# Down products of an FFN's last two tiles by blocks of tokens, and three RMS/layer norms worked block by block

## What is computed

```python
def swiglu(x, w_gu, w_down):
    gate, up = jnp.split(x @ w_gu, 2, axis=-1)
    return (jax.nn.silu(gate) * up) @ w_down
...
    h = h + 0.5 * swiglu(rms_norm(h, ffn1_norm[l]), ffn1_w_gu[l], ffn1_w_down[l])
    ...
    h = h + 0.5 * swiglu(rms_norm(h, ffn2_norm[l]), ffn2_w_gu[l], ffn2_w_down[l])
return rms_norm(h, final_norm)
...
x = post_norm(x, 0.5 * swiglu_2(x, ffn1_w_in[i], ffn1_w_out[i]), ln_g[i, 0], ln_b[i, 0])
```

## Time and profile before

| | |
|---|---|
| median of 3 runs | 1808.95 us (1808.13 to 1809.66) |
| the profiled execution | 1820.9 us, of which its span 1819.6 us |
| mean granted TensorE clock | 0.97 of full speed |
| PE busy | 1721.6 us, 95% of the span |
| DVE busy | 1193.8 us, 66% |
| ACT busy | 878.9 us, 48% |
| POOL busy | 92.3 us, 5% |
| DMA | 301.59 MB, mean 166 GB/s |

### The profile page before, as it was taken

One profiled execution on the slowest core, in us unless ns is written; L12 is line 12 of the kernel. 1 busy time (PEld: TensorE's weight loads), 2 busy tenths in 40 slices (PEclk: granted clock), 3 DMA queues, 4 the chain that ended last, 5 costly groups with the idle time before them and its releaser, 6 DMA issues.

```text
span 1819.6 us, 24706 instructions
## 1 busy us (share of the span) xinstructions
PE 1721.6 (95%) x9936; PEld 1489.1 (82%) x9936; DVE 1193.8 (66%) x1949; ACT 878.9 (48%) x1507; POOL 92.3 (5%) x123
## 2 busy tenths in 40 slices
PE   7999998989999999989999999799998998999995
PEld 6888897878888888888778888688888887888884
DVE  5766658837666666655757666666666674576665
ACT  5444546545444544455545454454443564454453
POOL 0000002210000000002210000100000000100000
PEclk9999998999999999999989999899998998999997
DMA  8545362025545454444425545355544232464531
GB/s 340 203 178 199 116 237 112 36 93 197 202 180 198 172 199 183 161 156 150 157 102 219 203 179 185 127 186 191 185 173 150 106 115 99 155 229 184 193 131 46
DMA packets 31970, 301.59 MB, mean 166 GB/s; under 512 B 3808, under 2 KB 4336, under 8 KB 5872
## 3 DMA queue, kind: packets, MB, share of 16 engines
q1 hardware_dynamic: 31856, 300.01, 44.8%
HBM read 298.93 MB, written 1.06 MB: 165 GB/s over the span
## 4 chain that ended last, share of the span: by engine, by line
PE 82%; DVE 10%; ACT 5%; issue 1%; POOL 1%; DMA 0%; SPq 0%; DVEq 0%; ACTq 0%
PE bank L402 28%; PE bank L392 25%; PE bank L391 11%; PE bank L381 7%; DVE w_lo L354 3%; PE bank L394 2%; ACT w_hi L347 1%; DVE x L663 1%; POOL rstd L771 1%; DVE x L687 1%; PE bank L434 1%; PE bank L448 1%; PE bank L449 1%; PE bank L964 1%; PE bank L1392 1%
## 5 line engine op out<-in xcount | busy, mean ns | idle before, releaser
L354 DVE TENSOR_TENSOR w_lo<-w_raw,w_hi 128x1024 fp32r<-128x1024 f32 (+5 forms) x545 | 607.1, 1165 | 265.3 <-ACT w_hi L347 265.1
L392 PE MATMUL bank<-xT,w_hi 128*128 128x512 f32 x1920 | 674.1, 396 | 1.0 <-DVE w_lo L354 0.9
L347 ACT ACTIVATE w_hi<-w_raw 128x1024 fp32r<-128x1024 f32 (+5 forms) x561 | 523.8, 995 | 150.1 <-PE bank L402 127.9
L391 PE MATMUL bank<-xT,w_lo 128*128 128x256 f32 x1680 | 468.5, 279 | 0.0
L392 PEld LDWEIGHTS bank<-xT,w_hi 128*128 128x128 f32 x1920 | 351.6, 188 | 71.1 <-DVE w_lo L354 1.7
L391 PEld LDWEIGHTS bank<-xT,w_lo 128*128 128x128 f32 x1680 | 316.7, 189 | 10.4
L619 ACT ACTIVATE ff_silu<-ff_silu 128x256 f32<-128x256 f32 x120 | 50.4, 420 | 389.1 <-DVE ff_silu L731 389.1
L402 PE MATMUL bank<-w_hi,hT_hi 128*128 128x512 f32 x528 | 206.1, 390 | 1.0 <-DVE hT_lo L740 1.0
L402 PE MATMUL bank<-w_hi,hT_lo 128*128 128x512 f32 x528 | 205.5, 389 | 0.0
L402 PE MATMUL bank<-w_lo,hT_hi 128*128 128x512 f32 x528 | 205.4, 389 | 0.0
L731 DVE TENSOR_REDUCE ff_silu<-bank 128x256 f32<-128x512 f32 x120 | 82.9, 691 | 110.0 <-PE bank L392 110.0
(11 more groups left out here) (332 smaller groups left out, 2172.3 us busy)
## 6 DMA issues: line engine op xcount, KB each, us to landing
w_raw<-in_ffn_a SPq DMA_DIRECT2D x22, 1536.0 KB, 6.7
w_raw<-in_ffn_b SPq DMA_DIRECT2D x22, 1536.0 KB, 6.6
w_raw<-in_ffn_c SPq DMA_DIRECT2D x22, 1536.0 KB, 6.5
w_raw<-in_ffn_d SPq DMA_DIRECT2D x22, 1536.0 KB, 6.6
w_raw<-in_ffn_e SPq DMA_DIRECT2D x22, 1536.0 KB, 6.5
w_raw<-in_ffn_f SPq DMA_DIRECT2D x22, 1536.0 KB, 6.5
gains<-in_gains SPq DMA_DIRECT2D x11, 1024.0 KB, 4.8
w_raw<-in_mla_up SPq DMA_DIRECT2D x8, 1280.0 KB, 5.7
```

The source lines that it names most:

```text
L347: nc.scalar.activation(hi, src, ACTF.Copy).then_inc(w_hi_made, 1)
L354: nc.vector.tensor_tensor(lo, src, hi.bitcast(F32), ALU.subtract).then_inc(w_lo_made, 1)
L391: nc.tensor.matmul(o[:, 0:SEQ], lo[:, c], xT[:, k, 0, :], start=False, stop=False)
L392: ins = nc.tensor.matmul(o, hi[:, c], xT[:, k, :, :], start=(k == 0), stop=(k == KD - 1))
```

## The change

```diff
-BY_BLOCKS = (7,)
+BY_BLOCKS = (1, 3, 4, 7)
...
                 if n in BY_BLOCKS:
-                    pe_warm((0, 0, 13, 0)[p])
+                    pe_warm(((0, 0, 13, 0) if n == 7 else (13, 2, 3, 0))[p])
                 elif n not in PLE_NORM:
                     pe_warm(({9: 20}.get(n, 13 if n >= 4 else 10), 3, 2, 0)[p])
...
-            down(FF_TILES - 2, 1)
-            down(FF_TILES - 2, 0)
             for b in range(TB):
+                down(FF_TILES - 2, b)
                 for ins in down(FF_TILES - 1, b):
                     ins.then_inc(acc_made, 1)
...
+            def add_ffn(n, b):
+                dve_add(n, b, 0.5)
+                if n >= 4:
+                    dve_minus_mean(n, b)
+
             dve_ffn(0, dve_lower_bound)
-            add_blocks(1, 0.5)
-            dve_turn(1, to_xn, RMS_EPS)
+            dve_turn_blocks(1, lambda b: add_ffn(1, b), to_xn, RMS_EPS)
             dve_mixer()
             add_blocks(2, 1.0)
             dve_turn(2, to_xn, RMS_EPS)
             dve_ffn(1)
-            add_blocks(3, 0.5)
-            dve_turn(3, in_place, RMS_EPS)
+            dve_turn_blocks(3, lambda b: add_ffn(3, b), in_place, RMS_EPS)
             dve_ffn(2)
-            add_blocks(4, 0.5)
-            dve_turn(4, dve_ln_apply, LN_EPS)
+            dve_turn_blocks(4, lambda b: add_ffn(4, b), dve_ln_apply, LN_EPS)
```

## The result

The changed kernel takes **1834.3 us** (median of 4 executions, 1829.64 to 1836.09) against 1809.31 for the kernel before, run beside it (4 executions, 1808.13 to 1812.05). The ratio is 1.0132, with a 95% interval of 1.011 to 1.0154. So it is slower, as forecast, by some 24 us (the ratio's excess; the two medians differ by 25) where 17.6 were forecast, and 1834.3 lies 1.8 us above the top of the range. The same kernel was run once more among the last experiments, beside 21 executions of the kernel before: 1836.12 against 1813.75, ratio 1.0117 [1.0095, 1.014], some 21 us (17 to 25; the medians differ by 22).

A forecast was written before the change was run, and what follows sets the result against it. The kernel was taken to wait for PE nearly everywhere (82% of the chain). Longer chains in three norms, 11.6 us, plus low clock, 6.0, made 17.6 on the median of 1808.95: 1826.5 us, range 1817 to 1832.5.

The forecast's parts named there:

- Block 0's lead: Rival: block 1's chain runs alone behind its last bank in norms 1, 3 and 4; faster, 1803.5 us; chance 0.04.
- The chain, 11.6 forecast: Front products later by 3.9 us in norm 1, 3.1 in norm 3; norm 4's back part 4.6 later.
- norm 4's front: Front products behind norm 4's first half of block 1, forecast to begin at 800.85.
- The clock, 6.0 forecast: Low clock behind PE's waits for block 1 in norms 1, 3 and 4: 2.0 us lost in each.
- The rival that the clock would hold: Clock holds in one or more of norms 1, 3, 4; 11.6 to 15.6 us slower, 1820.5 to 1824.5; chance 0.23.
- I cost this at nothing: FFN ends: PE's longer waits for tile 21's h, 1.9 us in two FFNs, 0.6 to 0.7 in four, priced zero.
- The cover I named: DVE reaches block 1's bank late at the FFN ends, hiding later down products; without it, 5.6 us.
- the thirteen fillers: Norm 1, ahead of the first transpose: 2.90 us, PE done at about 207, then waiting for block 1 until 209.8.
- The rival with the chance of 0.12: Hole at the FFN's end costs 3 to 5 us more than forecast: 1829.5 to 1831.5 us; chance 0.12.
- 1.2 us of copies: Norm 1: ACT copies between its last square and DVE's next mean, forecast to show in the changed profile.

The follow-up runs named there:

- e5: e2 with ACT squaring and copying block 0 before squaring block 1 in norms 1, 3 and 4; 1827.72 us, ratio 1.0079 to the kernel before.
- e6: e2 with DVE adding both blocks before block 0's mean in norms 1, 3 and 4; 1825.08 us, ratio 1.0068 to the kernel before.
- e2: The changed kernel with the old order of down products, norms 1, 3 and 4 by blocks; 1833.24 us, ratio 1.011 to the kernel before.
- e10: The kernel before with the new order of down products in the last four FFNs only; 1814.83 us against 1813.75, ratio 1.0009.
- e7: e2 with 14, 18 and 26 fillers instead of 3 ahead of block 1's first transpose in norms 1, 3, 4; 1829.95 us, ratio 1.0086.
- e4: The changed kernel with eight fillers in the hole ahead of tile 21's down products in the first two FFNs; 1831.98 us, ratio 1.0106.
- e1: The kernel before with the new order of down products in all six FFNs, norms as before; 1818.57 us against 1813.43, ratio 1.0029.
- e9: The kernel before with the new order of down products in the first two FFNs only; 1820.59 us against 1813.75, ratio 1.0036.
- e11: The changed kernel run again, unedited, beside the kernel before; 1836.12 us against 1813.75, ratio 1.0117.
- e3: The changed kernel without the thirteen fillers ahead of the first transpose in norms 1 and 3; 1833.03 us, ratio 1.0111 to the kernel before.
- e12: e6 with 12, 12 and 17 fillers instead of 3 ahead of block 1's first transpose in norms 1, 3, 4; 1824.74 us, ratio 1.0063.

## Why the prediction was off

**Right: the direction and the mechanism of the norms.** "Block 0's lead" buys a mean 0.34 us sooner and nothing else, because the front products need block 1 in either order, and block 1 pays for it in DVE's and ACT's queues. e5 and e6 each take back one part of that payment, 3.8 and 5.2 of the 12.9 us by which the three fronts are late in e2.

**The chain, 11.6 forecast.** With the old down products (e2) the three fronts begin 4.2, 3.0 and 5.75 us later than in the trace of before; forecast were 3.9 and 3.1, and for norm 4's front, 800.85 against 795.6, 5.2. Each is within 0.6 us. That norm 3 comes out so close is in part luck: the forecast was made against a trace whose norm 3 was late by 0.8 us (front at 8.5, in e10 at 7.7). Norm 4's extra is its transpose at the low clock, 1.12 us where the earlier trace rows has 0.66.

**The clock, 6.0 forecast.** All three fronts of the changed kernel began at 0.50, and filling the waits gave back 5.9 us in the traces (e7). The rival that the clock would hold, with a chance of 0.23, fell. The Trainium skill (TensorE: Matmul & The Clock Gate, Part 1 on the HAM clock gate) has the halved clock as the default that activity releases, and these three fronts, each behind a wait of PE, agree with it. For the slow start of a kernel it puts the penalty at under 1% of a typical span, and advises against fitting a count of slow matmuls. No run here measures that start; the clock's falls inside this kernel are not to be left out, with 0.7% between the fastest and the slowest execution of one kernel (1807.8 to 1819.85) and 1.2% to 1.3% for the whole change.

**The step that failed: "I cost this at nothing",** of the down products' hole. The cover I named was DVE, which is late there and in the new order takes block 1 later still. With the new order of DVE it did hide the products themselves: in e4, at full clock, norm 1's front came only 0.35 us later than in e2. (With the old order, in e1 and e9, it did not: 1.2 us.) What it did not hide was the clock: behind 1.87 us of waiting the granted clock fell to 0.54, block 1's down products took nearly twice their time, and then the thirteen fillers, with which I had PE done at about 207, stood at a lowered clock ahead of a transpose whose input had been ready for 5 us. In the first profile that made 3.0 us of front in norm 1 (e2 against the changed kernel), 3.4 us at the norm's end; in the second (e11) 1.4 and 0.7 us. The rival with the chance of 0.12 had this hole in it, but priced only the down products and the additions behind them, forgot the fillers between them and the transposes, and so ended at 1831.5; its 3 to 5 us on top of the 17.6 come nearest to the runs. On the kernel before, the new order of down products costs 5 to 6.5 us (e1, e9), clear of noise. Added to 17.6 that makes 22.6 to 24.1, and the measured differences are 21 and 24. On top of the new norms its price was not measured clear of noise: the changed kernel's ratios, 1.0117 and 1.0132, stand 1.3 and 4 us above e2's 1.011. That the hole costs something rests on e1, e9 and the two traces of the changed kernel; its size on top of the new norms stays open, between some 1 and 4 us.

**The base.** The three executions shown of before had a median of 1808.95; the 13, 13 and 21 executions beside the experiments gave 1813.4 to 1813.75. Against the last of these the changed kernel is 21 us slower. The base moves the forecast's time and not its difference, so it does not explain the 24 measured side by side. The spread of 12 us in one kernel is as large as the chain's whole term, and a range of 15 us about the forecast had little room for it.

**Points of the forecast of the profile:** additions 4.5 us apart (4.6 forecast), 1.2 us of copies (seen: 1.27 idle of DVE in norm 3), fronts at 11.8 and 15.9, clock near 0.5 at the head of all three fronts, and a hole of 1.9 us: as seen. Not foreseen: norm 1's fillers, and norm 8's shorter wait.

**Open.** In the profiles of e1 and e9 the clock held behind the hole of 1.87 us, in those of the changed kernel, twice, and of e3 it fell. What decides that was not found. Nor is it shown where e9's 4 us of clock lie, or why e12's median lacks what its trace gains at the norms, since almost every kernel has one profile and the falls move from execution to execution. ACT by blocks (e5) and all additions first (e6) were not run together, nor with block 1's mean ahead of block 0's low parts; whether an order by blocks with all three comes up to the kernel before is open.

## What to carry to other kernels

Ordering work by blocks pays only if some consumer can start on the first block alone, and then every engine of the chain must follow the new order; one that keeps its own (here ACT with both squares ahead of the copies) makes block 0's lead block 1's delay. Before taking independent matmuls out from under a wait, price the wait's effect on what runs behind it, fillers included: a filler sized for the full clock stands in the way when the clock has fallen. Where PE waits for about 2 us on a chain of other engines, products of the identity in that wait are cheap to try; in the kernel before, those in four places were together worth 4.5 us (1.5 to 7.4), most visibly at the two gates. Count them by the wait: seventeen in norm 4 of e12 held up the transpose that they stood ahead of.

## What was not expected of the hardware

- The clock fell while PE was busy without a gap: 0.54 from 199.4 to 204.4, after a wait that had ended at 197.6. With the wait filled (e4) the same products ran at 1.00, as they also did in e1 and e9 with the wait open. A wait's price can fall due after the wait.
- The same wait has both outcomes, in different executions: behind 2.09 us at norm 8 the clock fell in four of seven traces, behind 1.87 us in the first FFN in three of five; behind 1.27 us at norm 8 it held in all six.
- The time of one kernel follows its mean granted clock from execution to execution: 1807.8 us at 0.982, 1813.75 at 0.977, 1819.85 at 0.972 (correlation over the 21 executions -0.92).
